# Low parts of the down rows in the feed-forward loop: from VectorE to GpSimd

## The chip, the core and the metric

The kernel runs on one core of a Trainium2 chip. The time is what the device takes for one execution, in microseconds (us); of several runs the median counts. TensorE (PE) multiplies, VectorE (DVE), ScalarE (ACT) and GpSimd (POOL) work element by element, SyncE (SP) issues most of the DMAs.

## What is computed

The program is two networks, one after the other, for 256 positions of 1024 values: a first block (long convolution, neighbourhood attention, a gather of experts) and then two layers of a second block (attention, a state-space branch, a feed-forward part). Only the feed-forward part is touched by the change:

```python
def conv_glu_ffn(h, w_up, conv_w, conv_b, w_down):
    u = causal_dwconv(h @ w_up, conv_w, conv_b)       # 3 taps; 1024 -> 2 x 2816
    gate, val = u[..., :FFN_DIM], u[..., FFN_DIM:]
    return (jax.nn.silu(gate) * val) @ w_down         # 2816 -> 1024
```

All values are float32.

## The kernel before

**Split products.** A float32 product is made of three faster ones. A weight and an activation are each written as a high part and a low part (the remainder), and TensorE adds high x high, high x low and low x high. A chunk of weights is 128 partitions x 1024 values. For each chunk SyncE issues a DMA into one of six places of `wring`; ScalarE makes the high part by a copy with rounding into `w_hi` (`weights_high`, L1509); then someone makes the low part, `wring - w_hi`, into `w_lo`. `w_hi` and `w_lo` have four places each, so ScalarE starts on chunk n when TensorE is done with chunk n - 4. SyncE refills a place of `wring` when the low part of the chunk in it is there.

**Who makes the low part.** A table, `low_turn`, written once ahead of all engines, names "vector" or "pool" for each chunk and its count. The engine named does the work: VectorE (`weights_low`, L1993) as one operation over 1024 columns, GpSimd (`weights_low` further down, L2944 and L2946) as two over 512 columns each. Each engine raises a semaphore of its own, and `low_done` tells a waiting engine which one and what count. Before the change VectorE makes those of the feed-forward part (except one up chunk of each layer, the third, which GpSimd makes) and GpSimd most others.

**The loop.** Each of the two layers has 44 up chunks and 22 down rows; each down row is a chunk too. The loop over c has 11 iterations: four up chunks (two of the gate, two of the value), then, from c = 1, the two down rows 2c - 2 and 2c - 1. The last two down rows follow after the loop. TensorE takes the weights in just this order. For an up chunk it makes 8 products of 512 columns (high weight, both parts of the input) and 8 of 256 columns into one of four PSUM banks. For a down row it makes 12 products of 512 columns into four other banks, which collect over all 22 rows.

**Around it**, for each up chunk n: ScalarE copies one half of the result (L1946), VectorE adds the other (L2878, one input from PSUM), ScalarE makes the first tap (L1958), VectorE two more (L2891, twice; two inputs from SBUF). For each pair of gate and value ScalarE takes the silu (L1967), VectorE multiplies (L2907), ScalarE makes the high part of the product (L1939) and VectorE the low part (L2871). TensorE waits for the last of these (`glu_ready`) before a down row.

**The order.** Each engine has its own stream of instructions in fixed order. Where in its stream an engine converts a chunk is set by `SplitStream`: ahead of each wait for a group of products it does all chunks whose places are free by then. So on VectorE and ScalarE the conversions stand between the steps above; GpSimd has no other work in the two loops.

Of the kernel before, what the change touches and what calls it, by code (L numbers as in the profile page):

```python
# [436 lines left out]
def build(nc, d, where, out):  # L437
# [7 lines left out]
    wplan = weight_order(turn)  # L445
# [86 lines left out]
    second_block = [w[0] for w in wplan].index("w2_qkv")  # L532
# [3 lines left out]
    lo_ready_v = S("weights_lo_ready_vector")  # L536
    low_turn, low_counts = {}, {"pool": 0, "vector": 0}
    for n_, c_ in enumerate(split_chunks):
        who = "vector" if wplan[c_][0] in ("w2_up", "w2_dn") or 0 <= c_ - second_block < 2 else "pool"
        who = "pool" if wplan[c_][0] == "w2_up" and wplan[c_][2] == 2 else who  # L540
        low_counts[who] += 1
        low_turn[n_] = (who, low_counts[who])
# [2473 lines left out]
```

How the kernel before makes its waits and increments, by code:

```python
    def settle(self):  # L433
        self.eng.wait_ge(*self.last)
# [158 lines left out]
    def wait_filled(eng, name, i):  # L593
        due(eng, name, i)
        eng.wait_ge(psum_filled, turn[(name, i)] + 1)
# [4 lines left out]
    def wait_read(eng, name, i):  # L600
        due(eng, name, i)
        eng.wait_ge(*read_value(name, i))
# [217 lines left out]
    def finish(sp):  # L820
        for t in range(TT):
            sp.wait_ge(S("out_ready"), t + 1)
            sp.dma_start(out[:, t, :], x[:, t, :]).then_inc(S("out_stored"), 16)
        sp.wait_ge(S("out_stored"), 16 * TT)
# [2 lines left out]
    @block.sync  # L827
# [9 lines left out]
                sp.dma_start(arena[:, A_R + f4_at:A_R + hyw_n], d["hyw"][:, f4_at:hyw_n]).then_inc(S("f4_in"), 16)  # L837
                sp.dma_start(hyc[:, decay_at:hyc_n], d["hyc"][:, decay_at:hyc_n]).then_inc(S("decay_in"), 16)
            if c == 8:
                sp.dma_start(hyc[:, dft_at:inverse_at], d["hyc"][:, dft_at:inverse_at]).then_inc(S("dft_in"), 16)
                sp.dma_start(consts[:], d["consts"]).then_inc(S("consts_in"), 16)
            if c == 12:
                sp.dma_start(x[:], d["x"].rearrange("p (a b) -> p a b", b=D)).then_inc(S("x_in"), 16)
            if c == first_hyena + RING:
                sp.dma_start(hyc[:, inverse_at:decay_at], d["hyc"][:, inverse_at:decay_at]).then_inc(S("hyc_in"), 16)
            if second_block <= c < second_block + RING:
                sp.wait_ge(S("pair_used"), wring_freed(c % RING))
                sp.wait_ge(S("pair_dot"), PICKS - 1)
            if c >= RING:
                if c - RING in split_turn:
```

## Time and profile before

| | us |
|---|---|
| median of 3 runs | 2175.14 (2170.1 to 2175.27) |
| profiled execution | 2179.34 |
| its span | 2177.5 |
| TensorE busy | 1963.4 |
| VectorE busy | 1388.4 |
| ScalarE busy | 1041.5 |
| GpSimd busy | 1043.0 |

The profile records one execution. The time of the profiled execution holds 1.8 us around its span; it is 4.2 us above the median. Start times count from the start of the span. The two loops run from about 1424 to 1604 and from about 1987 to 2171. Busy time says who works, not who is waited for; for that the order in time is read.

### The profile page before, as it was taken

The numbers are of one execution on the slowest core, as the hardware profiler recorded it, in microseconds if no ns is written. First come the engines' busy times: TensorE is split into PE (matmuls) and PEld (weight loads), VectorE is DVE, ScalarE is ACT, GpSimd is POOL, SyncE is SP. The second block draws the span as 40 slices with busy tenths as digits, with TensorE's granted clock in tenths as the row PEclk, the third lists the DMA queues.
The fourth block names the chain that finished last, engine by engine and source line by source line (L and its number), as shares of the span: only waits on it lengthen the run. The fifth ranks groups of instructions, "written<-read, shape, count | busy, mean of one in ns | idle before, by whom it ended". The sixth has DMA issues, their size and how long they took to land.

```text
span 2177.5 us, 26297 instructions
## 1 busy us (share of the span) xinstructions
PE 1963.4 (90%) x9022; PEld 1437.5 (66%) x9022; DVE 1388.4 (64%) x2870; ACT 1041.5 (48%) x1957; POOL 1043.0 (48%) x844
## 2 busy tenths in 40 slices
PE   7999988887787678888999999999999999999998
PEld 3967767633333233333699787788879977788887
DVE  5768765676676776665277642378854775326887
ACT  4514545321221122211546686466664568846665
POOL 1723677654444344442787467700048865782000
PEclk9999999999999999999999999999999999999999
DMA  8523774899999999999654354545545535454553
GB/s 334 178 76 131 263 251 148 348 421 421 421 421 421 422 422 421 421 421 375 206 180 159 127 174 155 178 151 199 182 161 175 180 126 169 149 181 153 195 193 107
DMA packets 111733, 534.27 MB, mean 245 GB/s; under 512 B 12528, under 2 KB 12912, under 8 KB 78320
## 3 DMA queue, kind: packets, MB, share of 16 engines
q1 hardware_dynamic: 68112, 248.18, 34.2%
q0 software_dynamic: 38720, 275.96, 30.8%
q10 hardware_dynamic: 4768, 8.46, 1.3%
q8 instruction: 72, 1.18, 0.2%
q14 instruction: 61, 0.50, 0.1%
HBM read 531.43 MB, written 1.11 MB: 245 GB/s over the span
## 4 chain that ended last, share of the span: by engine, by line
PE 57%; DMA 22%; ACT 7%; DVE 6%; issue 4%; POOL 2%; ACTq 0%; SPq 0%; DVEq 0%; POOLq 0%
PE psum L894 55%; DMA arena<-in_peer_uv,arena 10%; DMA pair_rows<-in_peer_uv,arena 8%; DMA wring<-in_peer_uv,arena 3%; PE psum L973 2%; ACT w_hi L1509 2%; ACT arena L1520 1%; DVE arena L2891 1%; POOL w_lo L2946 1%; POOL w_lo L2944 1%; ACT arena L1884 1%; DVE w_lo L1993 1%; DMA x_rows<-in_x 0%; ACT arena L1892 0%; DVE dve_junk L2878 0%
## 5 line engine op out<-in xcount | busy, mean ns | idle before, releaser
L894 PE MATMUL psum<-w_hi,a_parts 128*128 128x512 f32 (+1 forms) x2112 | 673.1, 394 | 22.0 <-POOL w_lo L2946 11.7
L2944 POOL TENSOR_TENSOR w_lo<-wring,w_hi 128x512 fp32r<-128x512 f32 x282 | 375.8, 1333 | 509.3 <-ACT w_hi L1509 498.3
L1509 ACT ACTIVATE w_hi<-wring 128x1024 fp32r<-128x1024 f32 (+1 forms) x414 | 431.7, 1053 | 283.6 <-PE psum L894 247.5
L894 PE MATMUL psum<-a_parts,w_hi 128*128 128x256 f32 (+1 forms) x1952 | 484.4, 330 | 11.2 <-DVE a_parts L2587 7.5
L894 PEld LDWEIGHTS psum<-w_hi,a_parts 128*128 128x128 f32 x2112 | 396.6, 189 | 118.0 <-POOL w_lo L2946 15.4
L894 PE MATMUL psum<-w_lo,a_parts 128*128 128x512 f32 (+1 forms) x1056 | 409.6, 388 | 0.0
L2946 POOL TENSOR_TENSOR w_lo<-wring,w_hi 128x512 fp32r<-128x512 f32 x282 | 396.3, 1405 | 0.0
L894 PE MATMUL psum<-arena 128*128 128x512 f32 (+7 forms) x1148 | 332.3, 452 | 70.3 <-ACT arena L1755 47.0
L894 PE MATMUL psum<-a_parts,w_lo 128*128 128x256 f32 (+1 forms) x1344 | 377.5, 281 | 0.0
L894 PEld LDWEIGHTS psum<-a_parts,w_hi 128*128 128x128 f32 x1952 | 332.4, 193 | 44.8 <-issue 7.8
L894 PEld LDWEIGHTS psum<-arena 128*128 128x128 f32 (+2 forms) x1148 | 183.4, 198 | 201.9 <-issue 119.6
L894 PE MATMUL psum<-pair_rows,arena 128*128 128x512 f32 x512 | 250.0, 637 | 58.4 <-ACT arena L1755 58.4
L894 PEld LDWEIGHTS psum<-a_parts,w_lo 128*128 128x128 f32 x1344 | 259.8, 193 | 0.7
L894 PEld LDWEIGHTS psum<-pair_rows,arena 128*128 128x128 f32 x512 | 101.3, 202 | 200.5 <-issue 122.1
L894 PEld LDWEIGHTS psum<-w_lo,a_parts 128*128 128x128 f32 x1056 | 199.7, 189 | 41.9 <-issue 3.9
L2988 POOL DMA_INDIRECT pair_rows<-in_peer_uv,arena x128 | 137.0, 1071 | 167.3 <-PE psum L894 160.1
L1750 ACT ACTIVATE arena<-arena 128x4 f32<-128x4 f32 (+2 forms) x69 | 14.3, 207 | 337.7 <-DVE arena L2547 337.7
L1993 DVE TENSOR_TENSOR w_lo<-wring,w_hi 128x1024 fp32r<-128x1024 f32 x132 | 158.5, 1223 | 22.1 <-ACT w_hi L1509 17.8
L1755 ACT ACTIVATE arena<-consts,arena 128x128 f32<-128x128 f32 x256 | 82.4, 390 | 143.2 <-DVE arena L2504 143.0
L2988 POOL DMA_INDIRECT arena<-in_peer_uv,arena x80 | 87.5, 1093 | 104.0 <-PE psum L894 99.9
L894 PE MATMUL psum<-wring,arena 128*128 128x512 f32 x192 | 99.4, 668 | 27.6 <-ACT arena L1755 27.6
L1520 ACT ACTIVATE arena<-psum 128x512 f32<-128x512 f32 (+1 forms) x170 | 81.9, 521 | 66.0 <-PE psum L894 46.0
(266 smaller groups left out, 2096.9 us busy)
## 6 DMA issues: line engine op xcount, KB each, us to landing
wring<-in_w_up SPq DMA_DIRECT2D x88, 512.0 KB, 4.0
wring<-in_w_xbc SPq DMA_DIRECT2D x48, 512.0 KB, 4.1
wring<-in_w_dn SPq DMA_DIRECT2D x44, 512.0 KB, 3.8
wring<-in_w_adaT SPq DMA_DIRECT2D x32, 512.0 KB, 4.5
wring<-in_w_qkv SPq DMA_DIRECT2D x32, 512.0 KB, 3.6
wring<-in_w_z SPq DMA_DIRECT2D x32, 512.0 KB, 3.8
wring<-in_w_g SPq DMA_DIRECT2D x32, 512.0 KB, 3.8
wring<-in_w_ps SPq DMA_DIRECT2D x32, 512.0 KB, 3.9
```

The lines of the kernel that those rows point to most:

```text
L894: mm = lambda o, a, b, start, stop: nc.tensor.matmul(o, a, b, start=start, stop=stop, skip_group_check=True)
L973: m = nc.tensor.transpose(o[0:s.shape[-1], j * n:(j + 1) * n], s, ident[0:n, 0:n])
L1509: a.reaches(A(w_hi[:, n % SPLIT_RING, 0:width], wring[:, c % RING, 0:width], ACT.Copy), hi_ready, n + 1)
L1520: a.reaches(A(out_, in_, func, **kw), *read_value(name, i))
L1750: a.reaches(A(pact[:, cols_q], pdot[:, cols_q], ACT.Gelu), S("gelu_ready"), q + 1)
L1755: a.reaches(A(diag[:, n % (2 * BATCH), :], ident, ACT.Copy, scale=pw[:, n % TOPK:n % TOPK + 1]), S("diag_ready"), n + 1)
L1884: a.done(A(Lm[:, i % 2, (4 * half + j) * P:(4 * half + j + 1) * P], rows[:, j * P:(j + 1) * P], ACT.Relu, bias=acs_s[:, h:h + 1], scale=-1.0))
L1993: v.reaches(T.tensor_tensor(w_lo[:, r, 0:width], wring[:, c % RING, 0:width], w_hi[:, r, 0:width].bitcast(F32), ALU.subtract), *low_done(n))
L2891: ins = T.scalar_tensor_tensor(out=o[:, j:SEQ], in0=part[:, 0:SEQ - j], scalar=V(f"fcw{l}", 2 * FT * (2 - j) + col), in1=o[:, j:SEQ], op0= ...
L2944: nc.gpsimd.tensor_tensor(w_lo[:, r, 0:half], wring[:, c % RING, 0:half], w_hi[:, r, 0:half].bitcast(F32), ALU.subtract)
L2946: nc.gpsimd.tensor_tensor(w_lo[:, r, half:width], wring[:, c % RING, half:width], w_hi[:, r, half:width].bitcast(F32), ALU.subtract).then_ ...
L2988: pool.indirect_dma_start(out=pair(n), out_offset=None, in_=d["peer_uv"], in_offset=bass.IndirectOffsetOnAxis(ap=pidx[:, g, j:j + 1], axis ...
```

## The change

The table of who makes the low parts names VectorE no longer for the down rows, so that they fall to GpSimd, which makes them in two halves. The up chunks stay with VectorE (the third of each layer with GpSimd, as before).

```diff
     for n_, c_ in enumerate(split_chunks):
-        who = "vector" if wplan[c_][0] in ("w2_up", "w2_dn") or 0 <= c_ - second_block < 2 else "pool"
+        who = "vector" if wplan[c_][0] == "w2_up" or 0 <= c_ - second_block < 2 else "pool"
         who = "pool" if wplan[c_][0] == "w2_up" and wplan[c_][2] == 2 else who
```

The streams of TensorE and ScalarE keep their instructions and order. On VectorE 44 operations fall away. In the iteration c = 1 of the first layer (U4 to U7, then the first two down rows) two of them stood between other steps:

```order
 L1993 TENSOR_TENSOR w_lo<-wring,w_hi 128x1024
-L2878 TENSOR_TENSOR dve_junk<-psum,dve_junk 128x256
-L1993 TENSOR_TENSOR w_lo<-wring,w_hi 128x1024
-L2878 TENSOR_TENSOR dve_junk<-psum,dve_junk 128x256
+L2878 TENSOR_TENSOR dve_junk<-psum,dve_junk 128x256 x2
 L2891 SCALAR_TENSOR_TENSOR arena<-dve_junk,cols,arena 128x255
 L2891 SCALAR_TENSOR_TENSOR arena<-dve_junk,cols,arena 128x254
 L2871 TENSOR_TENSOR a_parts<-arena,a_parts 128x256 x2
-L1993 TENSOR_TENSOR w_lo<-wring,w_hi 128x1024
 L2878 TENSOR_TENSOR dve_junk<-psum,dve_junk 128x256
```

The low part of the first down row stood between two L2878, that of the second behind L2871; both are gone and the rest moves up.

At the end of a layer's loop VectorE's stream was this, from the gated values of the last but one pair on:

```order
1725 L2871 TENSOR_TENSOR a_parts<-arena,a_parts 128x256 x2
1726 L1993 TENSOR_TENSOR w_lo<-wring,w_hi 128x1024
1727 L2878 TENSOR_TENSOR dve_junk<-psum,dve_junk 128x256
1728 L2891 SCALAR_TENSOR_TENSOR arena<-dve_junk,cols,arena 128x255
1729 L2891 SCALAR_TENSOR_TENSOR arena<-dve_junk,cols,arena 128x254
1730 L1993 TENSOR_TENSOR w_lo<-wring,w_hi 128x1024
1731 L2878 TENSOR_TENSOR dve_junk<-psum,dve_junk 128x256
```

and, after the four taps and two L2907 that are the same in both, it ended so:

```order
1736 L2907 TENSOR_TENSOR arena<-arena 128x256 x2
1737 L2871 TENSOR_TENSOR a_parts<-arena,a_parts 128x256 x2
1738 L1993 TENSOR_TENSOR w_lo<-wring,w_hi 128x1024
1739 L2858 TENSOR_TENSOR x_rows<-x_rows,psum 128x512 x3
```

It is now:

```order
1696 L2871 TENSOR_TENSOR a_parts<-arena,a_parts 128x256 x2
1697 L2878 TENSOR_TENSOR dve_junk<-psum,dve_junk 128x256
1698 L2891 SCALAR_TENSOR_TENSOR arena<-dve_junk,cols,arena 128x255
1699 L2891 SCALAR_TENSOR_TENSOR arena<-dve_junk,cols,arena 128x254
1700 L2878 TENSOR_TENSOR dve_junk<-psum,dve_junk 128x256
1701 L2891 SCALAR_TENSOR_TENSOR arena<-dve_junk,cols,arena 128x255
1702 L2891 SCALAR_TENSOR_TENSOR arena<-dve_junk,cols,arena 128x254
1703 L2891 SCALAR_TENSOR_TENSOR arena<-dve_junk,cols,arena 128x255
1704 L2891 SCALAR_TENSOR_TENSOR arena<-dve_junk,cols,arena 128x254
1705 L2907 TENSOR_TENSOR arena<-arena 128x256 x2
1706 L2871 TENSOR_TENSOR a_parts<-arena,a_parts 128x256 x2
1707 L2858 TENSOR_TENSOR x_rows<-x_rows,psum 128x512 x3
```

Three low parts (D19, D20 and D21, the last behind the final gated values) have left this stretch. GpSimd's stream gains 22 pairs L2944, L2946 in a row in each of the two loops. SyncE's refills behind a down row now wait for GpSimd's semaphore:

```order
 L855 DMA wring<-in_w_dn 128x1024 [waits weights_lo_ready_vector]
 L855 DMA wring<-in_w_up 128x1024 [waits weights_lo_ready_vector] x4
+L855 DMA wring<-in_w_dn 128x1024 [waits weights_lo_ready] x2
+L855 DMA wring<-in_w_up 128x1024 [waits weights_lo_ready_vector] x4
+L855 DMA wring<-in_w_dn 128x1024 [waits weights_lo_ready] x2
```

The order of the DMAs stays; every two refills by down rows wait for another engine.

## Rows read from the trace of the kernel before

**Rows 1.** The instructions of lines L1993 and L2944: duration min/median/max in ns.
```profile
L1993 DVE TENSOR_TENSOR w_lo<-wring,w_hi x132: 1215/1219/1552, 1043.5 to 2163.9; 128x1024 fp32r<-128x1024 f32 x132
L2944 POOL TENSOR_TENSOR w_lo<-wring,w_hi x282: 1067/1292/2259, 47.5 to 1975.1; 128x512 fp32r<-128x512 f32 x139, 128x416 fp32r<-128x416 f32 x2
```

**Rows 2.** Busy time in one iteration of the second layer's loop.
```profile
core 0: us, PE busy (x) PEld busy (x) DVE busy (x) ACT busy (x) POOL busy (x), PEclk, DMA share, GB/s
2083.24:2100.03 16.79, 16.79 (x90) 14.31 (x89) 13.89 (x22) 10.64 (x19) 0.00 (x0) 1.00 0.57 189
```

**Rows 3.** Waits in three iterations, 2083.24 to 2133.62: total us, times, longest.
```profile
DVE dve_junk L2878 <- ACT dve_junk L1946: 5.3, 7, 0.8
...
DVE w_lo L1993 <- ACT w_hi L1509: 1.4, 3, 0.5
```

**Rows 4.** Order in time, one iteration: start us, us, engine, line, [idle before].
```profile
2100.91 1.23 DVE L1993 TENSOR_TENSOR w_lo<-wring,w_hi 128x1024 fp32r<-128x1024 f32 x1 [0.45 <-ACT w_hi L1509]
...
2104.58 0.76 DVE L2871 TENSOR_TENSOR a_parts<-arena,a_parts 128x256 fp32r<-128x256 f32 x2
...
2112.56 3.49 DVE L1993 TENSOR_TENSOR w_lo<-wring,w_hi 128x1024 fp32r<-128x1024 f32 x3
...
2107.82 0.40 PE L894 MATMUL psum<-w_hi,a_parts 128*128 128x512 f32 x1
...
2116.14 0.40 PE L894 MATMUL psum<-a_parts,w_hi 128*128 128x512 f32 x1
```

**Rows 5.** Order in time, VectorE beside GpSimd's halves in earlier stages.
```profile
124.56 2.94 DVE L2076 TENSOR_TENSOR dve_junk<-arena 128x256 f32<-128x256 f32 x2
...
128.88 0.75 DVE L2076 TENSOR_TENSOR dve_junk<-arena 128x256 f32<-128x256 f32 x2
...
124.35 1.44 POOL L2944 TENSOR_TENSOR w_lo<-wring,w_hi 128x512 fp32r<-128x512 f32 x1 [12.46 <-ACT w_hi L1509]
125.76 1.47 POOL L2946 TENSOR_TENSOR w_lo<-wring,w_hi 128x512 fp32r<-128x512 f32 x1
...
1308.24 2.26 POOL L2946 TENSOR_TENSOR w_lo<-wring,w_hi 128x512 fp32r<-128x512 f32 x1
1309.29 0.67 DVE L2803 TENSOR_TENSOR arena<-arena,psum 128x512 f32<-128x512 f32 x1
```

**Rows 6.** Order in time, second iteration of the first layer's loop.
```profile
1437.73 1.05 ACT L1509 ACTIVATE w_hi<-wring 128x1024 fp32r<-128x1024 f32 x1
...
1440.20 1.23 DVE L1993 TENSOR_TENSOR w_lo<-wring,w_hi 128x1024 fp32r<-128x1024 f32 x1
...
1443.06 0.76 DVE L2871 TENSOR_TENSOR a_parts<-arena,a_parts 128x256 fp32r<-128x256 f32 x2
...
1451.04 3.48 DVE L1993 TENSOR_TENSOR w_lo<-wring,w_hi 128x1024 fp32r<-128x1024 f32 x3
...
1452.31 0.49 PE L894 MATMUL psum<-a_parts,w_hi 128*128 128x512 f32 x1 [0.18 <-DVE w_lo L1993]
```

**Rows 7.** Order in time, the end of the second layer's loop.
```profile
2154.14 1.05 ACT L1509 ACTIVATE w_hi<-wring 128x1024 fp32r<-128x1024 f32 x1
...
2156.36 1.05 ACT L1509 ACTIVATE w_hi<-wring 128x1024 fp32r<-128x1024 f32 x1
...
2160.96 1.04 ACT L1509 ACTIVATE w_hi<-wring 128x1024 fp32r<-128x1024 f32 x1
...
2154.96 0.76 DVE L2871 TENSOR_TENSOR a_parts<-arena,a_parts 128x256 fp32r<-128x256 f32 x2
...
2160.20 2.04 DVE L2891 SCALAR_TENSOR_TENSOR arena<-dve_junk,cols,arena 128x255 f32<-128x255 f32 x4
...
2163.18 0.76 DVE L2871 TENSOR_TENSOR a_parts<-arena,a_parts 128x256 fp32r<-128x256 f32 x2
2163.86 1.22 DVE L1993 TENSOR_TENSOR w_lo<-wring,w_hi 128x1024 fp32r<-128x1024 f32 x1
...
2165.23 0.47 PE L894 MATMUL psum<-w_hi,a_parts 128*128 128x512 f32 x1 [1.36 <-DVE w_lo L1993]
```

## The prediction

> **What bounds the kernel now.** I read the costliest groups first: VectorE makes the low part of a chunk in one operation (1.22 us), GpSimd in two halves with a median of 1.29 us each [rows 1]. Then the busy time of one iteration of the feed-forward loop: TensorE is busy for all of its 16.79 us, VectorE for 13.89, GpSimd for nothing [rows 2]. So TensorE bounds the loop, and VectorE has 2.90 us per iteration free. The waits over three iterations say what these are: 5.3 + 1.4 us, or 2.2 per iteration, are true waits for ScalarE; the rest (0.7) is gaps between operations [rows 3]. TensorE has no line among the waits there. Last the order in time at the two ends of a layer's loop, where TensorE does wait [rows 6, 7].
>
> I call the up chunks U0 to U43 and the down rows D0 to D21 of a layer. TensorE's order is U4 to U7, D0, D1, U8 to U11, D2, D3 and so on, and U40 to U43, D18 to D21 at the end.
>
> **What is removed and added.** VectorE loses 44 operations; the loop issues three in 3.49 us, so one is worth 1.15 [rows 4], 50.6 us in all. Two up chunks had their low part on GpSimd in both versions. GpSimd gains 88 halves. One starts 1.25 us behind the other when nothing hinders them (1.29 less the 0.04 by which one overlaps the next, as in [rows 5], 124.35 + 1.44 against 125.76), so a chunk takes 2.5. The DMA queue and TensorE wait for the same event, counted by another semaphore; nothing else is queued on GpSimd in these loops. TensorE and ScalarE issue the same work.
>
> **In the middle of a layer: nothing.** In the iteration of 2100 the high part of the first down row is done just before 2100.91, where VectorE now starts the low part; TensorE first needs it at 2107.82 [rows 4]. GpSimd is done at about 2103.4, 4.4 us early, and VectorE's next operation on two SBUF operands that matters comes after that. The second down row falls elsewhere: its high part is ready as VectorE works on L2871 at 2104.58 [rows 4], and from there it has L2878, then two L2891.
>
> Here a second effect counts. In [rows 5] two operations of VectorE with two inputs in SBUF, 0.75 us together when alone (128.88), take 2.94 at 124.56, with two GpSimd halves beside them at 1.44 and 1.47 instead of 1.29. At 1308.24 a half takes 2.26 because VectorE is at work. The durations fit one picture: only one of the two works at a time, and they take turns, an operation each. An operation of VectorE with an input from PSUM is not held: 0.67 us at 1309.29, beside that half. So a GpSimd half costs VectorE up to 1.25 us, and a chunk up to 2.2 as measured at 124.56, 2.5 if the halves meet no gap; the saving is 1.15.
>
> For the second down row of the iteration: half 1 holds the second L2871 by 1.2, L2878 then runs beside half 2, and half 2 holds L2891 by 0.8. 2.0 less the saved 1.15 is +0.9. VectorE thus comes to the three low parts of the next up chunks at 2113.4 instead of 2112.56; the first is done at 2114.6, and TensorE needs it at 2116.14 [rows 4]. 1.5 us of slack are left of 2.4. After it VectorE waits for ScalarE anyway and has caught up. TensorE stays bound, its time unchanged. The DMA queue refills a down row's place some 1.3 to 1.8 us later, and ScalarE reads what lands there a whole iteration later.
>
> The Trainium skill says the same with a harder word: in SBUF — State Buffer, section SBUF: two separate sides, the pair of ports that VectorE and GpSimd share is an exclusive lock, held for a whole instruction by the one that started first, and VectorE takes it for two SBUF inputs. It does not say who comes next; the turns are this trace's. Without that lock the ends of the layer below would come out as a gain of about 2 us in all; with it they are a loss.
>
> **At the start of a layer's loop: +1.4 us, twice.** In the second iteration VectorE works without a wait and is late: the low part of U9, begun at 1451.04, releases TensorE at 1452.31, after an idle time [rows 6]. Whatever delays VectorE before it is TensorE's time. The high part of D0 is done at 1438.78 (1437.73 + 1.05). GpSimd's first half then runs beside two L2878, which read PSUM, in the place of the operation at 1440.20: free. The second half holds the second L2891, and D1's two halves hold the two L2871 (1443.06) [rows 6]: 3 x 1.25 = 3.75, less two operations of 1.15, is +1.45. The bounds are -0.2 (all four halves hidden, TensorE's idle of 0.18 gone) and +2.7 (all four in full). I take +1.4, since VectorE has no pause there. In the next iteration TensorE is 1.4 later too, and U13 is just in time by my walk. The other layer has the same picture.
>
> **At the end: +2.8 us, twice.** Before, TensorE starts D20 and D21 at 2165.23, when VectorE has made D21's low part at 2163.86, behind the last gated values (L2871 at 2163.18) [rows 7]. That operation goes away, -1.15 for what stands behind it. But D19, D20 and D21 now come one after the other on GpSimd, beside the last taps. I walk through it with 1.25 for a half, 0.4 to 0.5 for a VectorE operation:
> D19's high part is done at 2155.19: half 1 until 2156.6, between the two L2871; half 2 2156.95 to 2158.2, L2878 beside it; L2891 to 2158.7. D20 (high part long done, 2157.41): half 1 to 2159.9, L2891 to 2160.4, half 2 to 2161.65 with L2878 beside it, where VectorE was ready for the four L2891 at 2160.20 before. Those begin at 2161.65. D21's high part is done at 2162.9, 0.9 later than before (2160.96 + 1.04), because ScalarE waits for L2878. Half 1 2163.2 to 2164.4, L2891, half 2 2164.9 to 2166.15. Only then L2907 twice, ScalarE's two copies and L2871: glu ready at 2167.9, TensorE off at 2168.0. 2168.0 - 2165.23 = +2.8. The bounds: -0.6 (no turn lost, D21's low part 2.5 behind its high part at 2162.0, so TensorE at 2164.6) and +3.7 (no L2878 of 0.45 under a half, twice). I take +2.8: the row at 124.56 is of the same size of operation, back to back, and lost the whole 2.2.
>
> **Sum.** 2 x (1.4 + 2.8) = +8.4 us. The profiled execution is 2179.34 us with a span of 2177.5; it becomes 2187.7. It was 4.2 above the median of the runs (2175.14), so the median becomes about 2183.5, +0.39%. The saved 50.6 us of VectorE were, but for the ends, never on the path.
>
> **Rivals.**
> 1. *Part of the turns is lost only* (+3 to +6, 2178 to 2181). GpSimd might slip into gaps between VectorE's operations, which sum to 0.7 us per iteration, or the tail might order itself better than my walk. For it: my walk is exact to some 0.3 us per turn, and one turn less is 1.25. Against: rows 5 show full turns.
> 2. *Not slower: the ends get shorter* (the other side). Place: D19 to D21. If the halves lie where VectorE waits, TensorE gains 0.6 to 1.4 us at each tail and 0.2 at each start: -1.6 to -3.2, about 2173. It decides from the point at which fewer than two of the tail's six halves hold VectorE. Against: ready times in [rows 7] fall into the densest part of VectorE's work. The Trainium skill's GPSIMD Engine Reference, 4.1 Engine selection, calls elementwise work on two inputs about 2x slower on GpSimd; 2.5 against 1.15 agrees, and that alone would leave this rival standing, as 4.4 us of slack take it.
> 3. *VectorE becomes the bound in the middle.* If all four halves held it, an iteration would cost it 5.0 - 2.3 = 2.7 us more, against 2.2 of true waits [rows 3]: 0.5 us per iteration, 20 iterations, +10 on top, 2190 to 2194. For it: VectorE starts the layer late. Against: the first down row lies in a pause.
> 4. *It does not do what it says* (the scheduler's order hides it): the order shows the halves on GpSimd, so 1 in 50.
>
> **Chances.** Forecast 0.52 (2181 to 2186); rival 1 0.18; rival 2 0.13; rival 3 0.15; rival 4 0.02. A measurement tells about 0.3%, 6.5 us, from no change. Slower by more: most of the forecast's own range and rival 3, 0.44 + 0.14 = 0.58. Within: the rest of the forecast, rivals 1, 4 and most of 2, 0.39. Faster: 0.03. The range 2173 to 2189 leaves out half of rival 2 and most of rival 3, 0.18. It holds 2181.7, the edge of "same".
>
> **What would show it.** Right: L1993 88 times; L2891, L2871 and L2907 with means above 0.48 and 0.42 us at the second down row only; GpSimd halves of up to 1.7 us; TensorE busy without a gap in the middle; the low part of U9 about 1.4 us later against its layer's start, and an idle of about 4 us before D20, released by VectorE (L2871) or GpSimd. Wrong: operations of VectorE at their old length beside halves (no turns); TensorE waiting in every iteration (rival 3); or an idle before D20 below 1.4 us (rival 2).

## The result, and the profile after

| | before | after |
|---|---|---|
| median of 8 runs each (us) | 2175.27 | 2184.95 |
| lowest to highest (us) | 2170.1 to 2179.45 | 2180.4 to 2191.68 |
| ratio, 95% interval | | 1.0047 [1.0034, 1.0061] |
| span of the profiled execution (us) | 2177.5 | 2182.4 |
| low parts: VectorE L1993, GpSimd L2944 | 132, 282 | 88, 326 |

The changed kernel is 0.47% slower, 9.7 us at the medians; the forecast was 2183.5 us. The two spans differ by 4.9 us only. The loops of the changed kernel's execution began 5.2 us earlier (its first L2878 stood at 1422.6 instead of 1427.8), in work that the edit doesn't touch; from there to the end of the span it took 759.8 us, that of before 749.7. Either profile is one execution, and that of before lies 4.1 us above the median of its runs, that of the changed kernel 0.6 below. So the places are compared against the start of their own loop.

The instructions of single lines of the changed kernel come first: line, engine, number, duration min/median/max in ns, first and last start.

```profile
L2891 DVE SCALAR_TENSOR_TENSOR arena<-dve_junk,cols,arena x176: 482/484/1580, 1424.9 to 2164.2; 128x255 f32<-128x255 f32 x88, 128x254 f32<-128x254 f32 x88
...
L2871 DVE TENSOR_TENSOR a_parts<-arena,a_parts x44: 410/426/1548, 1438.9 to 2168.0; 128x256 fp32r<-128x256 f32 x44
```

44 operations have left VectorE, as the edit says (132 less 88). The medians of L2891 and L2871 are what they were; the longest of each is over three times as long (before: 489 and 428 ns). Some operations were held, most were not.

Next, TensorE's waits over the whole trace, the lines of the feed-forward loops and of what follows them: us in total, times, longest. (Lines of other stages moved by 1 to 2 us between the two profiles as well, in work that the edit doesn't touch.) The kernel before:

```profile
PE psum L894 <- DVE w_lo L1993: 4.4, 5, 1.4
...
PE psum L973 <- DVE arena L2020: 0.9, 1, 0.9
```

and the changed kernel:

```profile
PE psum L894 <- DVE a_parts L2871: 8.0, 4, 2.6
...
PE psum L973 <- DVE arena L2020: 1.9, 1, 1.9
```

Only four waits on the gated values make up the 8.0 us, in 44 down rows. They stand at D0 and at D20 of either layer. In order of time, TensorE in the changed kernel:

```profile
1440.35 0.47 PE L894 MATMUL psum<-w_hi,a_parts 128*128 128x512 f32 x1 [1.39 <-DVE a_parts L2871]
...
1599.79 0.50 PE L894 MATMUL psum<-w_hi,a_parts 128*128 128x512 f32 x1 [2.63 <-DVE a_parts L2871]
...
1607.38 1.10 PE L973 MATMUL psum<-consts,arena 128*128 128x128 f32 x8 [1.85 <-DVE arena L2020]
...
2008.99 0.47 PE L894 MATMUL psum<-w_hi,a_parts 128*128 128x512 f32 x1 [1.35 <-DVE a_parts L2871]
...
2168.48 0.52 PE L894 MATMUL psum<-w_hi,a_parts 128*128 128x512 f32 x1 [2.62 <-DVE a_parts L2871]
```

In this fence the first and the fourth are the starts, the second and the fifth the tails; between a start and its tail TensorE has no idle time. The tail's 2.62 us answers to the 1.36 of [rows 7], so a tail lost 1.26 by waiting. The third is the normalisation of the rows behind the first layer (L2020), for which TensorE waited 0.91 us before.

At the start of the first layer, VectorE and GpSimd in order of time:

```profile
1435.67 3.12 DVE L2891 SCALAR_TENSOR_TENSOR arena<-dve_junk,cols,arena 128x255 f32<-128x255 f32 x2
1438.94 1.60 DVE L2871 TENSOR_TENSOR a_parts<-arena,a_parts 128x256 fp32r<-128x256 f32 x2
...
1433.68 2.03 POOL L2944 TENSOR_TENSOR w_lo<-wring,w_hi 128x512 fp32r<-128x512 f32 x1 [22.53 <-ACT w_hi L1509]
1435.67 1.30 POOL L2946 TENSOR_TENSOR w_lo<-wring,w_hi 128x512 fp32r<-128x512 f32 x1
1437.22 1.29 POOL L2944 TENSOR_TENSOR w_lo<-wring,w_hi 128x512 fp32r<-128x512 f32 x1 [0.25 <-ACT w_hi L1509]
1438.47 1.45 POOL L2946 TENSOR_TENSOR w_lo<-wring,w_hi 128x512 fp32r<-128x512 f32 x1
```

These GpSimd rows are D0 and D1, two halves each. D0's first half is itself held: it takes 2.03 us, 0.74 more than alone, beside a low part that VectorE had begun at 1433.34 (L1993, 1.22 us). The two L2891 and the two L2871 behind it are held by the other three.

Why D20 is late is seen on VectorE and GpSimd at the end of the second layer, in order of time (the times are 2.0 us later than those of [rows 7] by what happened before):

```profile
2158.75 0.41 DVE L2878 TENSOR_TENSOR dve_junk<-psum,dve_junk 128x256 f32<-128x256 f32 x1
2159.31 2.38 DVE L2891 SCALAR_TENSOR_TENSOR arena<-dve_junk,cols,arena 128x255 f32<-128x255 f32 x2
2161.92 0.42 DVE L2878 TENSOR_TENSOR dve_junk<-psum,dve_junk 128x256 f32<-128x256 f32 x1 [0.22 <-DVE arena L2891]
2162.49 2.20 DVE L2891 SCALAR_TENSOR_TENSOR arena<-dve_junk,cols,arena 128x255 f32<-128x255 f32 x4
2164.72 2.80 DVE L2907 TENSOR_TENSOR arena<-arena 128x256 f32<-128x256 f32 x2
2167.44 0.98 DVE L2871 TENSOR_TENSOR a_parts<-arena,a_parts 128x256 fp32r<-128x256 f32 x2
...
2157.26 1.29 POOL L2944 TENSOR_TENSOR w_lo<-wring,w_hi 128x512 fp32r<-128x512 f32 x1 [1.38 <-ACT w_hi L1509]
2158.51 1.48 POOL L2946 TENSOR_TENSOR w_lo<-wring,w_hi 128x512 fp32r<-128x512 f32 x1
2159.94 1.47 POOL L2944 TENSOR_TENSOR w_lo<-wring,w_hi 128x512 fp32r<-128x512 f32 x1
2161.38 1.47 POOL L2946 TENSOR_TENSOR w_lo<-wring,w_hi 128x512 fp32r<-128x512 f32 x1
2164.37 1.47 POOL L2944 TENSOR_TENSOR w_lo<-wring,w_hi 128x512 fp32r<-128x512 f32 x1 [1.52 <-ACT w_hi L1509]
2165.79 1.44 POOL L2946 TENSOR_TENSOR w_lo<-wring,w_hi 128x512 fp32r<-128x512 f32 x1
```

The GpSimd rows are D19, D20 and D21, two halves each. The first two L2891 take 2.38 us together instead of 1.01, beside D19's second half and D20's first. L2878, with an input from PSUM, keeps its 0.41. The four L2891 beside the end of D20's second half take 2.20 instead of 2.04, since the half is nearly over when they begin. Both L2907 are held by D21's halves: 2.80 instead of 0.76. All GpSimd pays for these turns is some 0.18 us per half (1.47 instead of 1.29).

The last view is the busy time in stretches of 2 us; the eighth column, behind the five engines, is the clock granted to TensorE, as a share of 2.4 GHz:

```profile
1607.00:1609.00 2.00, 1.10 (x8) 0.86 (x8) 1.34 (x4) 1.15 (x5) 2.00 (x3) 1.00 0.47 135
1609.00:1611.00 2.00, 1.66 (x4) 1.42 (x5) 1.71 (x7) 1.97 (x8) 0.69 (x1) 0.51 0.61 176
1611.00:1613.00 2.00, 2.00 (x7) 1.54 (x7) 1.08 (x5) 0.90 (x1) 1.02 (x1) 0.64 0.62 236
...
2168.00:2170.00 2.00, 1.52 (x4) 1.27 (x5) 0.42 (x1) 1.47 (x2) 0.00 (x0) 0.71 0.00 0
2170.00:2172.00 2.00, 2.00 (x6) 1.53 (x5) 0.69 (x1) 0.11 (x1) 0.00 (x0) 0.50 0.00 0
2172.00:2174.00 2.00, 2.00 (x9) 1.60 (x9) 0.69 (x1) 1.06 (x4) 0.00 (x0) 0.94 0.00 0
```

Behind each layer's end the clock falls to 1.2 GHz, in the first layer behind the wait for the normalisation, in the second behind the tail's. What it lacks of full speed is 2.00 x (0.49 + 0.36) = 1.7 and 2.00 x (0.29 + 0.50 + 0.06) = 1.7 us, so either fall lasted some 3.4 us. In the kernel before it stays at 1.00 in both places. What the path lost by it is read from the rows. In the first layer, from TensorE's L973 behind the normalisation to VectorE's next group of eight L2587 it took 8.77 us (1607.38 to 1616.15) instead of 7.31, so 1.5. In the second the 24 products of D20 and D21 took 7.37 us instead of 5.74, so 1.6.

Put together against the kernel before: the start costs what the way from a loop's first L2891 to the idle time in front of D20 became longer, 172.28 us (1424.88 to 1597.16) instead of 170.66, and 172.35 instead of 171.05 in the second layer. So 1.6 and 1.3 us at the starts, 2 x 1.26 at the tails, 0.94 at L2020, 1.5 and 1.6 for the clock: 9.5 us, beside 9.7 at the medians and 10.1 between the two profiles. That it comes so near the medians is partly luck, since the clock's share is that of one execution.

### The profile page after: what moved, and what is told of

It is laid out like the page before. It is cut to its first block, busy times and chain, and to the rows that moved or that the text cites. A ratio compares the mean times of both kernels' runs of the same rounds, so it can differ in the third digit from the quotient of the medians.

```text
span 2182.4 us, 26341 instructions
## 1 busy us (share of the span) xinstructions
PE 1960.4 (90%) x9022; PEld 1432.7 (66%) x9022; DVE 1379.3 (63%) x2826; ACT 1040.1 (48%) x1957; POOL 1160.5 (53%) x932
## 3 DMA queue, kind: packets, MB, share of 16 engines
q8 instruction: 72, 1.18, 0.2%
## 4 chain that ended last, share of the span: by engine, by line
PE 58%; DMA 22%; ACT 6%; DVE 6%; issue 4%; POOL 3%; ACTq 0%; SPq 0%; DVEq 0%; POOLq 0%
PE psum L894 57%; DMA pair_rows<-in_peer_uv,arena 9%; DMA arena<-in_peer_uv,arena 8%; DMA wring<-in_peer_uv,arena 4%; PE psum L973 2%; POOL w_lo L2946 2%; ACT w_hi L1509 2%; POOL w_lo L2944 1%; ACT arena L1520 1%; DVE arena L2891 1%; DMA x_rows<-in_x 0%; ACT arena L1755 0%; ACT arena L1902 0%; ACT arena L1884 0%; DMA wring<-in_w_in 0%
## 5 line engine op out<-in xcount | busy, mean ns | idle before, releaser
L2944 POOL TENSOR_TENSOR w_lo<-wring,w_hi 128x512 fp32r<-128x512 f32 x326 | 437.8, 1343 | 582.8 <-ACT w_hi L1509 572.2
L2946 POOL TENSOR_TENSOR w_lo<-wring,w_hi 128x512 fp32r<-128x512 f32 x326 | 455.8, 1398 | 0.0
L894 PE MATMUL psum<-wring,arena 128*128 128x512 f32 x192 | 92.8, 630 | 24.4 <-ACT arena L1755 24.4
L1993 DVE TENSOR_TENSOR w_lo<-wring,w_hi 128x1024 fp32r<-128x1024 f32 x88 | 104.7, 1224 | 14.1 <-ACT w_hi L1509 10.7
```

The costliest lines, as they stand in the source:

```text
L894: mm = lambda o, a, b, start, stop: nc.tensor.matmul(o, a, b, start=start, stop=stop, skip_group_check=True)
L1993: v.reaches(T.tensor_tensor(w_lo[:, r, 0:width], wring[:, c % RING, 0:width], w_hi[:, r, 0:width].bitcast(F32), ALU.subtract), *low_done(n))
L2944: nc.gpsimd.tensor_tensor(w_lo[:, r, 0:half], wring[:, c % RING, 0:half], w_hi[:, r, 0:half].bitcast(F32), ALU.subtract)
L2946: nc.gpsimd.tensor_tensor(w_lo[:, r, half:width], wring[:, c % RING, half:width], w_hi[:, r, half:width].bitcast(F32), ALU.subtract).then_ ...
```

## Experiments

The first three experiments put a part of the down rows on GpSimd and leave the rest with VectorE, as before.

**1. Rows D2 to D17 alone.**

```diff
-        who = "vector" if wplan[c_][0] == "w2_up" or 0 <= c_ - second_block < 2 else "pool"
+        down = wplan[c_][0] == "w2_dn"
+        who = "vector" if (wplan[c_][0] == "w2_up" or 0 <= c_ - second_block < 2
+                           or (down and not (2 <= wplan[c_][2] < FT - 4))) else "pool"
```

> Only the down rows 2 to 17 of each layer have their low part on GpSimd; rows 0, 1 and 18 to 21 are back on VectorE. Turns theory: the middle of the loop has slack for what the turns cost, so the time is that of the kernel before, within 1 us (2175 or so), and TensorE waits as before (about 0.2 to 0.5 us at U9, 1.36 at D20), at full clock. Rival, VectorE is too full all through the loop: a loss of 3 us or more stays.

Measured 2177.97 us beside 2176.63, 1.0008 [0.9996, 1.002]. The gated values (L2873 in this kernel), one line's instructions:

```profile
L2873 DVE TENSOR_TENSOR a_parts<-arena,a_parts x44: 418/426/1543, 1439.9 to 2157.5; 128x256 fp32r<-128x256 f32 x44
```

Operations are held as long as in the changed kernel (1543 ns), and it can't be told from no change. TensorE is busy in the middle without a gap. So VectorE's reserve there takes 16 of 22 rows, with their turns, at no cost that the runs can tell (the interval ends at +4.4 us). There is no idle time at D0, and D20 waits 1.36 us in the first layer as before and 1.73 in the second. VectorE is not the bound of the middle: rival 3 is out.

**2. Rows D0 and D1 alone** (`wplan[c_][2] < 2` in the same place).

> Only the down rows 0 and 1 of each layer are on GpSimd. Turns theory: D0 starts 1.8 us late because L2871 is held, the old idle at U9 goes away: +1.3 to +1.5 us per layer, +2.8 in all. Rival, GpSimd's slowness as such or its semaphore: nothing, since both low parts are there before TensorE asks.

Measured 2178.2 us, 1.001 [1.0001, 1.0019]: +1.6 us at the medians, where +2.8 was expected; the interval, 0.2 to 4.1 us, holds both. TensorE's wait for the gated values:

```profile
PE psum L896 <- DVE a_parts L2873: 2.8, 2, 1.4
```

It is the start of the changed kernel alone (1.39 + 1.35 there), with the idle time in front of U9 gone in return. The clock stays up at both tails.

**3. Rows D18 to D21 alone** (`wplan[c_][2] >= FT - 4`).

> Only the down rows 18 to 21 of each layer are on GpSimd. Turns theory: TensorE idles 2.6 us instead of 1.36 before D20 in both layers (+2.5), the clock falls to half behind that for some 3 us in both (+3), and the normalisation behind the first layer's loop is held (+1): +6.5 in all. If the clock only fell by chance in the one profile: +3.5.

Measured 2181.76 us, 1.0036 [1.0024, 1.0048]: +5.1 us, where +6.5 was expected. TensorE's waits, with longest last:

```profile
PE psum L896 <- DVE a_parts L2873: 5.3, 2, 2.6
...
PE psum L975 <- DVE arena L2022: 1.9, 1, 1.9
```

The busy times in stretches of 2 us behind the first layer's end:

```profile
1608.00:1610.00 2.00, 1.13 (x7) 0.83 (x6) 1.14 (x5) 1.97 (x8) 1.72 (x2) 0.68 0.75 258
1610.00:1612.00 2.00, 2.00 (x6) 1.59 (x5) 1.97 (x7) 1.93 (x5) 0.00 (x0) 0.50 0.61 168
1612.00:1614.00 2.00, 2.00 (x6) 1.57 (x5) 0.11 (x1) 0.00 (x0) 1.99 (x2) 0.50 0.25 102
```

The tail's idle time, the held normalisation (L2022 in this kernel) and the lower clock all come with four rows of 22. The fall in these lines lasts twice as long as in the changed kernel: from TensorE's L975 to VectorE's group of eight L2589 it took 10.19 us (1607.40 to 1617.59), 2.9 more than in the kernel before. The three parts sum to 1.3 + 1.6 + 5.1 = 8.0 us, beside 9.7 for the whole; the intervals are wide enough for that difference.

**4. GpSimd issues the same operations, but they are tiny.** 16 of the 1024 columns are made, in two operations of 8; the rest of the down rows' low parts is left out.

```diff
+            if wplan[c][0] == "w2_dn":
+                total, pieces = 16, 2
+                piece = total // pieces
+                for j in range(pieces):
+                    at = slice(j * piece, (j + 1) * piece)
+                    ins = nc.gpsimd.tensor_tensor(w_lo[:, r, at], wring[:, c % RING, at],
+                                                  w_hi[:, r, at].bitcast(F32), ALU.subtract)
+                ins.then_inc(lo_ready, 1)
+                return
```

> GpSimd makes only 16 of the 1024 columns of each down row's low part (two operations of 8 columns); the rest of the computation of these low parts is left out. VectorE is relieved as in the change. Turns theory: without long halves nothing holds VectorE, and the ends get shorter: D20 starts without or with under 0.3 us of idle, 2 to 4 us faster than before (about 2172). Rival, the loss comes from the hand-over to another engine (semaphores, order): the loss of 9 us stays.

Measured 2171.12 us, 0.998 [0.9969, 0.9991], 5.5 us less than before; 2 to 4 were expected. The instructions of one line:

```profile
L2891 DVE SCALAR_TENSOR_TENSOR arena<-dve_junk,cols,arena x176: 482/484/489, 1422.3 to 2149.5; 128x255 f32<-128x255 f32 x88, 128x254 f32<-128x254 f32 x88
```

No L2891 is held, and there is no idle time at D0, U9 or D20. The wait for the normalisation in the first layer is there, though, and longer than before (1.55 us instead of 0.91), and the clock stays at 1.00 behind it. The engine, its semaphores and its place in the order are the same as in the changed kernel, so the loss lies in the time for which its operations run. 5.5 us is also what the low parts of the down rows cost in the kernel before, and about the most that this change could have gained (the interval is 2.0 to 6.7 us). 2.7 us of it are the idle times at D20 [rows 7]; the rest wasn't assigned.

**5 and 6. One operation of 1024 columns, and four of 256**, by `total, pieces = width, 1` and `width, 4` in the same edit.

> The changed kernel, with one GpSimd operation of 1024 columns for a down row's low part in place of two of 512. Turns theory (one engine at a time, an operation each): VectorE is held once for up to 2.4 us instead of twice for up to 1.2; the longest L2891 or L2871 goes from 1.58 us to about 2.9, the number of lengthened ones to about half, the time stays within 2 us of the changed kernel's. Rival, both engines share a bandwidth and slow each other in proportion: the longest L2891 stays near 1.6 us.

> The changed kernel, with four GpSimd operations of 256 columns for a down row's low part. Turns theory: the longest L2891 or L2871 falls from 1.58 us to about 1.2, but up to four are lengthened per row; each turn lets a VectorE operation through after 0.7 us, so GpSimd waits more and VectorE is held for as long in sum: within 2 us of the changed kernel. Rival, shared bandwidth: the longest stays near 1.6 us.

Measured 2187.77 us, 1.005 [1.0032, 1.0068], and 2179.07 us, 1.0013 [0.9999, 1.0026], beside 2176.16. The gated values with one operation, then with four:

```profile
L2871 DVE TENSOR_TENSOR a_parts<-arena,a_parts x44: 411/426/2664, 1441.0 to 2173.3; 128x256 fp32r<-128x256 f32 x44
...
L2871 DVE TENSOR_TENSOR a_parts<-arena,a_parts x44: 410/942/972, 1441.1 to 2168.2; 128x256 fp32r<-128x256 f32 x44
```

The longest follows the length of one GpSimd operation, some 2.4, 1.3 and 0.8 us: 2664 ns with one operation, 1548 with halves, 972 with quarters. With quarters more operations are held (the median rises to 942 ns), each for less. TensorE's waits for the gated values, with one operation and then with four:

```profile
PE psum L894 <- DVE a_parts L2871: 10.8, 4, 3.8
...
PE psum L894 <- DVE a_parts L2871: 4.6, 2, 2.3
```

Quarters have no wait at D0 and 2.3 at D20. Most of the change's loss is gone with quarters, where the expectation had the time within 2 us of the changed kernel's: it follows the length of one operation where VectorE has no reserve, though GpSimd makes the same columns. In the profile what is gone are the waits at D0, 0.3 us at each tail and one of the two falls of the clock. The longest VectorE operations, 2664, 1548 and 972 ns for the same columns, are the clearest test of the turns.

**7. The changed kernel with products that keep TensorE at work.** 16 products of 128 columns on a free PSUM bank stand before the wait for the gated values of D20, in each layer; they add work, and their results are not used.

```diff
+WARM = 16
...
+                    idle = bank(L + "up", 2 * FT - 4)
+                    wait_read(pe, L + "up", 2 * FT - 4)
+                    for j in range(WARM):
+                        mm(idle[:, 0:P], ident, ones, True, True)
                     pe.wait_ge(S("glu_ready"), FT * l + FT)
```

> The changed kernel with 16 small products of TensorE (128x128, about 0.13 us each, into a PSUM bank that is free) ahead of its wait for the last gated values in each layer; nothing reads them. If idle time is what lets the clock fall: at the second layer's end the clock stays at full speed (24 products in 5.7 us instead of 7.4), 1.6 us won; at the first layer's end the fall comes after a later idle and may stay. If the fall has another cause: no change there, 2185.

Measured 2183.42 us, 1.003 [1.0018, 1.0042]. TensorE in order of time at the second layer's end, the fill (its 16 products are 32 instructions) and then D20:

```profile
2163.53 3.73 PE L895 MATMUL psum<-consts 128*128 128x128 f32 x32
2167.02 0.48 PE L895 MATMUL psum<-w_hi,a_parts 128*128 128x512 f32 x1
```

A stretch there, with the clock in the eighth column (the next, 2170 to 2172, reads 1.00 too):

```profile
2168.00:2170.00 2.00, 2.00 (x10) 1.66 (x9) 0.69 (x1) 0.60 (x2) 0.00 (x0) 1.00 0.00 0
```

The clock stays at 1.00 at the second layer's end. But it also did in experiment 6, behind 2.3 us of idle time there, and in experiment 10 below, so one profile doesn't show that the fill did it. The fill takes some 3.3 us in place of 2.6 of idle time and so pushes D20 back by 0.7 (the gated values were there at 2166.28), and the fall behind the normalisation in the first layer stays. The gain on the changed kernel (1.003 against 1.0047) is within the two intervals. The experiment is inconclusive.

**8. The kernel before, with the last products in another order.** All of row 20's and 21's products waited for D21's low part because row 21 came second. Now D20 is applied to two outputs first.

```diff
-                    last_two = [take("w2_dn", l), take("w2_dn", l)]
-                    for n in DOWN_ORDER:
-                        for k, w in zip((FT - 2, FT - 1), last_two):
+                    last_two = {FT - 2: take("w2_dn", l)}
+                    first, second, third, fourth = DOWN_ORDER
+                    for k, n in ((FT - 2, first), (FT - 2, second), (FT - 1, first), (FT - 1, second),
+                                 (FT - 2, third), (FT - 1, third), (FT - 2, fourth), (FT - 1, fourth)):
+                        if k not in last_two:
+                            last_two[k] = take("w2_dn", l)
...
```

> The kernel before with TensorE's last two down rows in another order: row 20 for two of the four outputs first, which needs no low part of row 21, then row 21 for them. All low parts stay on VectorE. The 1.36 us that TensorE waits for row 21's low part at each layer's end go: -2.7 us in all, 2174 against 2176.6. If the wait was for the gated values instead: no change.

Measured 2175.38 us beside 2176.16, 0.999 [0.9979, 1.0001]; 2.7 us less were expected. The idle time of [rows 7], 1.36 us in either layer, is gone, but in the first layer the next thing takes it back. VectorE, its normalisation (L2024 in this kernel), and GpSimd beside it, in order of time:

```profile
1600.96 2.17 DVE L2024 TENSOR_SCALAR arena<-x_rows,small_values 128x512 f32<-128x512 f32 x2
...
1600.16 1.29 POOL L2948 TENSOR_TENSOR w_lo<-wring,w_hi 128x512 fp32r<-128x512 f32 x1
1601.41 1.44 POOL L2950 TENSOR_TENSOR w_lo<-wring,w_hi 128x512 fp32r<-128x512 f32 x1
```

GpSimd makes the low parts of the next layer's qkv chunks at that time, in the kernel before too. TensorE came earlier and met more of them; it waited 1.8 us for L2024 instead of 0.9, and the clock stood at 0.61 and 0.54 in the next two stretches of 2 us.

**9. The same, and the first two qkv chunks on VectorE**, so that no half stands beside the normalisation.

```diff
+        who = "vector" if wplan[c_][:2] == ("w2_qkv", 1) and wplan[c_][2] < 2 else who
```

> The kernel before with two edits: the order of the last two rows' products of the earlier experiment (row 20 for two outputs, row 21 for them, then the rest), and the low parts of the first two qkv chunks of the second layer on VectorE instead of GpSimd, so that no GpSimd half stands beside the normalisation (L2022 to L2024 there) at the end of the first layer. My theory, that a GpSimd half holds a VectorE operation with one input in SBUF as well: the normalisation's two-operation group is back at about 1.4 us from 2.17, TensorE's wait for it (1.81 us there) at about 0.9 or, with the two added low parts of 0.53 us each on VectorE ahead of it, up to 1.9; the clock then stays full or falls as before by what that wait becomes; time from 0.3 to 2.5 us under the kernel with the order alone (2175.4 beside 2176.2 of before), so 2173 to 2175. Rival, that the hold is VectorE's own queue and not GpSimd: the group stays at 2.2 us and the time at 2175.4.

Measured 2176.84 us beside 2176.69, 0.9998 [0.9987, 1.0008]. VectorE in order of time at the first layer's end:

```profile
1601.67 2.36 DVE L1998 TENSOR_TENSOR w_lo<-wring,w_hi 128x1024 fp32r<-128x1024 f32 x2 [0.90 <-ACT w_hi L1514]
1603.94 1.88 DVE L2863 TENSOR_TENSOR x_rows<-x_rows,psum 128x512 f32<-128x512 f32 x3
...
1606.88 0.88 DVE L2025 TENSOR_SCALAR arena<-x_rows,small_values 128x512 f32<-128x512 f32 x2
```

The normalisation (L2025) takes 0.88 us without a half beside it, against 2.17: GpSimd held it, although it has one input tensor in SBUF only (and one value per partition from `small_values`). In experiment 8 itself the pair that follows with no half beside it takes 0.88 as well. The gain was not there, for a reason that the expectation had too small: a chunk of 1024 columns costs VectorE 1.2 us, and two of them stand in front of the residual additions (L2863). TensorE's wait for the normalisation became 2.4 us, where at most 1.9 was expected. The mechanism is shown, the repair is not one.

**10. The changed kernel, with the other order of the last products** (the edit of experiment 8).

> The changed kernel with the order of the last two rows' products altered: row 20 for two outputs, row 21 for them, then the rest. In the kernel before, that order took away the tail's idle. My theory: in the changed kernel TensorE waits ahead of row 20 itself, for its activation (L2871, 2.62 us, made late by the halves beside D19 to D21), and the altered order doesn't move that: idle of 2.6 us at row 20 stays, the fall of the clock behind it too, and the time stays within 1.5 us of the changed kernel's, 1.0035 to 1.0055 of before. Rival, that the order of products is what decides the tail whoever makes the low parts: the idle falls below 1.4 us in both layers and the time to 1.002 or less.

Measured 2185.65 us beside 2176.69, 1.0048 [1.0031, 1.0066], as slow as the changed kernel. TensorE in order of time at D20 of either layer:

```profile
1601.45 0.72 PE L894 MATMUL psum<-w_hi,a_parts 128*128 128x512 f32 x1 [2.63 <-DVE a_parts L2875]
...
2169.15 0.50 PE L894 MATMUL psum<-w_hi,a_parts 128*128 128x512 f32 x1 [2.62 <-DVE a_parts L2875]
```

The stretches behind each of the two:

```profile
1603.00:1605.00 2.00, 2.00 (x7) 1.51 (x6) 0.00 (x0) 1.35 (x2) 1.52 (x2) 0.51 0.02 6
...
2170.00:2172.00 2.00, 2.00 (x10) 1.65 (x9) 0.48 (x1) 0.15 (x1) 0.00 (x0) 1.00 0.00 0
```

The idle times are the same to 0.01 us: what is late in the changed kernel are the gated values, ahead of any order of products. The clock, though, behaves otherwise. After the same 2.6 us of idle time it falls at once in the first layer here (0.72 us for the first product), and not at all in the second, where the changed kernel's fell. In the first layer it falls a second time behind the waits of 0.50 and 1.18 us at and after the normalisation.

## Why the prediction held, step by step

**Middle: nothing.** Right. TensorE is busy without a gap from D0 to the tail, and experiment 1 is at +1.3 us with an interval from -0.9 to +4.4.

**Start: +1.4, twice.** Right in size (1.6 and 1.3; experiment 2, with both starts alone, +1.6 with an interval from 0.2 to 4.1), a few microseconds off in place. The prediction let the delay run on until U9. It already shows at D0, where the gated values are wanted. Three turns were lost, as forecast, on slightly other operations: two L2891 took 3.12 us instead of 1.00, held by D0's second and D1's first half, and the pair of L2871 1.60 instead of 0.76, by D1's second. D0's first half cost VectorE nothing, as forecast, though it did not run beside two L2878: it met a low part of VectorE's and came 0.74 us late itself. U9's old idle time then vanished, since TensorE came later. The sum was the same because one delay was moved, not added.

**Tail: +2.8, twice.** The mechanism was right and the term was twice too large: 1.26, twice. The step that failed is the walk through D19 and D20, "with 1.25 for a half, 0.4 to 0.5 for a VectorE operation". Each turn of VectorE was put fully between two halves, so that D20's second half would end at 2161.65 and the four L2891 begin there. A half between turns takes 1.47 us instead of 1.29, 0.18 for the turn and not 0.4 to 0.5, and in the times of [rows 7] D20 was done at 2160.85 and the L2891 had begun at 2160.49. TensorE's idle time at D20 was 2.6 us, where the prediction's sign of being right was about 4. The number was there to be had: the halves at 124.35 and 125.76 are 1.44 and 1.47 long [rows 5]. The rest of the walk held: D21's two halves cost 2.04 at L2907, and 0.22 more at L2871.

**The normalisation, +0.94 in the first layer.** Not in the prediction. It took it that only operations with two inputs in SBUF are held, and it looked at the loop alone. Behind the tail stands L2020 with one input tensor in SBUF, and the halves of the next layer's qkv chunks run beside it. Experiments 8 and 9 show that they hold it: 2.17 and 0.88 us for the same pair. The prediction had passed over half of the page that it cites: the Trainium skill, SBUF — State Buffer, section SBUF: two separate sides, gives the lock also to a VectorE operation in a 2-port perf mode, and names `tensor_scalar` among those that can enter one. No trace here shows the mode, but the durations fit it: alone, L2020 makes 512 columns in 0.44 us, and L2858, as large and with an input from PSUM, takes 0.69.

**The clock, +3.1.** Not in the prediction, though the table of stretches was at hand. The two ends had 1.36 and 0.91 us of idle time at full clock; the change added to both. In the profiles of before and of experiments 1, 2 and 4, with nothing added at the tails beyond 0.4 us, the clock stays at 1.00 at both ends; in each of the others (after, 3, and 5 to 10), with longer waits at a tail or at the normalisation, it fell at one of them at least. That is a correlation over twelve profiles, and not a clean one: it stayed up behind waits of 1.73 us (experiment 1, second tail) and 1.55 (experiment 4, normalisation) and fell behind one of 1.41 (experiment 7, normalisation). The experiment meant to test it, 7, did not settle it. So that the added waits brought the clock down is argued, not shown.

**The sum.** +8.4 was forecast and 9.7 measured, so the time was right partly by luck, by terms that make up for each other: -3.1 in the tails, +0.9 and +3.1 for what wasn't seen, +0.1 at the starts. The forecast's case (the turns at both ends, nothing in the middle) is what happened. Rival 1 described the tail better than the forecast did, and rival 2 fell: VectorE was held in both tails.

**Open.** Why the clock falls after one idle time of 2.6 us and not after another of the same length isn't settled; the profiles show one execution each. The runs of a kernel lie up to 13 us apart, and how much of that is the clock was not tried.

## What to carry to other kernels

GpSimd's work is free only where VectorE has a reserve: what counts is not the sum of busy time, it is whether a VectorE operation on the path has to sit out a whole GpSimd operation. So give GpSimd short operations (quarters instead of halves took away some three quarters of the loss here), and leave to VectorE what falls due at the start and at the end of a loop, where experiments 2 and 3 found the cost that can be told from noise. That avoids the loss and gains nothing by itself (experiment 1): TensorE bounds the middle. And when an idle time of TensorE grows at the end of a stage, reckon with the clock behind it too: here the lower clock took 3.1 us, nearly as much as the added waits at the tails and at the normalisation (3.5), though it doesn't fall behind every such wait.

## What the hardware showed that was not expected

- An operation of VectorE with one input tensor in SBUF (TENSOR_SCALAR, 128x512) is held by a GpSimd half as well: 2.32 us for two in the changed kernel, 2.17 in experiment 8, 0.88 with GpSimd quiet. Those with an input from PSUM (L2878, 0.41 to 0.42 us) were never held.
- The two sides of a turn pay very differently: VectorE a whole operation of GpSimd (up to 1.1 us at halves, 2.2 at whole chunks, 0.6 at quarters), GpSimd 0.18 us beside operations of 256 columns. Where VectorE's operation had 1024 columns and had begun first, GpSimd lost more: 0.74 us at D0 (2.03 instead of 1.29).
- After idle times of 1.2 to 3.8 us TensorE ran at 1.2 GHz for about 3.4 us, at a cost of 1.5 to 1.7 us, though not after each of them; a fall can last twice that, as in experiment 3 (0.68, 0.50, 0.50, 0.61 in four stretches of 2 us), where it cost 2.9 us, and in experiment 5.
